# Parts of the samples' value product reordered, homes of their own for the first output weights, four bank pairs for the second layer's output

## The reference

```python
# layer 0: one input projection; branch A: GLU, causal depthwise convolution, layer norm, swish;
# branch B: attention with three parts (compressed blocks, chosen blocks, sliding window)
def nsa_block(q, g, ...):
    p_c = masked_softmax(q . kc);  o_c = p_c @ vc                 # compressed keys
    idx = top_k(score from p_c)                                    # 16 blocks of 64 keys
    p_s = masked_softmax(q . ks[idx]); o_s = p_s @ vs[idx]
    p_w = masked_softmax(q . kw, last 512); o_w = p_w @ vw
    return gq[0] * o_c + gq[1] * o_s + gq[2] * o_w
y0 = concat(A * silu(gate_a), B * silu(gate_b)) @ w_out_even      # 1024 x 1024
x1 = layer_norm(alpha * x + y0)
# layer 1: pooling mixer
v, gate = split(x1 @ w_in_odd)
d = causal window means of v (2, 4, 8, 16 tokens) - v
mixed = (d per group @ w_pool_grp) * scale
y = layer_norm(alpha * x1 + (mixed * silu(gate)) @ w_out_odd)      # 1024 x 1024
```

## Time and profile before

| | us |
|---|---|
| median of 3 runs | 1155.79 (1154.0 to 1157.73) |
| the profiled execution, its own time | 1155.27 |
| its span | 1153.5 |
| PE busy in it | 1107.2 (96%) |
| DVE, ACT, POOL busy | 739.5, 381.8, 369.4 |

### The profile page before, as it was taken

One profiled execution on the slowest core, in us unless ns is written; L12 is line 12 of the kernel. 1 busy time (PEld: TensorE's weight loads), 2 busy tenths in 40 slices (PEclk: granted clock), 3 DMA queues, 4 the chain that ended last, 5 costly groups with the idle time before them and its releaser, 6 DMA issues.

```text
span 1153.5 us, 17848 instructions
## 1 busy us (share of the span) xinstructions
PE 1107.2 (96%) x7080; PEld 918.1 (80%) x7080; DVE 739.5 (64%) x1337; ACT 381.8 (33%) x812; POOL 369.4 (32%) x376
## 2 busy tenths in 40 slices
PE   6999999999999989999999999899999999998997
PEld 6888999999988845556555556688799999997884
DVE  3677889999983598656555556556546620276745
ACT  4202111223223567766556655210121211362000
POOL 4544520000002587664754464300022221326000
PEclk9999999999999999999999999999999999998999
DMA  8653512253220122140572063722221111041321
GB/s 251 230 168 107 183 37 55 87 177 110 52 42 1 53 70 74 38 146 2 205 242 102 1 220 117 175 91 84 72 74 54 37 55 44 0 146 73 128 91 46
DMA packets 85884, 113.67 MB, mean 99 GB/s; under 512 B 21952, under 2 KB 67144, under 8 KB 85727
## 3 DMA queue, kind: packets, MB, share of 16 engines
q1 hardware_dynamic: 71849, 69.51, 19.7%
q0 software_dynamic: 11776, 41.95, 10.6%
q10 hardware_dynamic: 2182, 1.16, 0.4%
HBM read 100.91 MB, written 16.64 MB: 102 GB/s over the span
## 4 chain that ended last, share of the span: by engine, by line
PE 81%; DVE 7%; DMA 5%; POOL 3%; issue 2%; ACT 1%; SPq 1%; DVEq 0%; ACTq 0%
PE PS L697 25%; PE PS L1730 16%; PE PS L1908 15%; PE PS L1260 5%; PE PS L1246 5%; PE PS L1125 5%; PE PS L685 3%; PE PS L1163 2%; DMA RING<-in_cache_kv_sel,idx 2%; DMA WRAW<-in_w_in_even 2%; DVE PS L1342 1%; PE PS L1169 1%; DVE ACC L557 1%; PE PS L1888 1%; DMA WOR<-in_w_out_even 1%
## 5 line engine op out<-in xcount | busy, mean ns | idle before, releaser
L604 DVE SCALAR_TENSOR_TENSOR Y<-U,SM,Y 128x1024 f32<-128x1024 f32 x120 | 147.9, 1293 | 0.3
L697 PE MATMUL PS<-XH,WH 128*128 128x352 f32 (+1 forms) x648 | 146.5, 330 | 0.0
L697 PE MATMUL PS<-XL,WH 128*128 128x352 f32 (+1 forms) x648 | 143.6, 326 | 0.0
L697 PE MATMUL PS<-XH,WL 128*128 128x352 f32 (+1 forms) x648 | 142.9, 325 | 0.0
L697 PEld LDWEIGHTS PS<-XH,WH 128*128 128x128 f32 (+1 forms) x648 | 107.6, 185 | 2.7
L697 PEld LDWEIGHTS PS<-XH,WL 128*128 128x128 f32 (+1 forms) x648 | 107.9, 185 | 1.4
L697 PEld LDWEIGHTS PS<-XL,WH 128*128 128x128 f32 (+1 forms) x648 | 107.6, 185 | 1.4
L2015 POOL TENSOR_TENSOR WL<-WRAW,WH 128x1024 fp32r<-128x1024 f32 x14 | 37.8, 2698 | 216.2 <-ACT WH L1960 216.2
L557 DVE SCALAR_TENSOR_TENSOR ACC<-PS,SM,ACC 128x508 f32<-128x508 f32 x124 | 86.9, 741 | 25.1 <-PE PS L685 23.1
L288 POOL TENSOR_TENSOR WL<-WRAW,WH 128x1024 fp32r<-128x1024 f32 x12 | 28.7, 2390 | 231.8 <-ACT WH L361 231.8
L1730 PE MATMUL PS<-WOH,XH 128*128 128x512 f32 (+1 forms) x288 | 93.4, 407 | 6.3 <-DVE GT L2077 3.1
(11 more groups left out here) (319 smaller groups left out, 2065.0 us busy)
## 6 DMA issues: line engine op xcount, KB each, us to landing
WRAW<-in_w_in_even SPq DMA_DIRECT2D x16, 512.0 KB, 3.8
WRAW<-in_w_in_odd SPq DMA_DIRECT2D x16, 512.0 KB, 4.0
TM<-in_state_win_kv SPq DMA_DIRECT2D x12, 512.0 KB, 6.9
XIN<-in_x_prompt SPq DMA_DIRECT2D x8, 512.0 KB, 12.8
WRAW<-in_w_in_even SPq DMA_DIRECT2D x16, 256.0 KB, 3.8
XR<-in_x_prompt SPq DMA_DIRECT2D x8, 512.0 KB, 3.5
layer_out<-R SPq DMA_DIRECT2D x8, 512.0 KB, 2.6
XR<-layer_out SPq DMA_DIRECT2D x8, 512.0 KB, 3.3
```

The lines of the kernel that those rows point to most:

```text
L604: v.scalar_tensor_tensor(dst, src, CWT[:, i, t:t + 1], dst, ALU.mult, ALU.add).then_inc(s_cv, 1)
L697: ins = pe.matmul(PS[0:mcols, 3 * slot + c, 0:CH], w[:, slot, kk, 0:mcols], x[:, kk, c * CH:(c + 1) * CH], start=(kk == 0 and n == 0), sto ...
```

## The change

Three things. First, the six parts of "pv" are put in another order. Part 0 is now the compressed term, the window of the round's last two samples and the new tokens; parts 1 and 2 are the gathered quarters 2 and 3; part 3 is the window of the first two samples; parts 4 and 5 are the quarters gathered again. What waits for the parts moves with them: the gathers for 4 and 5 come behind parts 1 and 2, those for the next round behind parts 4 and 5, SP's reload of windows behind part 0, and that for the next round behind part 3. The planner's costs and dues are changed too. Second, the raw blocks of the first output weight get six homes (WOR0) in place of four: blocks 0 and 1 are loaded behind the last round's part 0, blocks 4 and 5 while the attention still runs, blocks 6 and 7 in the homes of 2 and 3 behind the end of it. Third, in the second layer's output a tile's banks come from four pairs, (6, 0, 2, 4), in place of two; tile 0 begins with four blocks in banks 6 and 7 without waiting for the gating, tile 1 with four in 0 and 1.

```diff
@@ attention planner
             def key_tile(b, i):
-                fill(("kt", b, i), 520, ("late", ("gather", a, i), 6000) if i < 4 else None)
+                fill(("kt", b, i), 520, ("late", ("gather", a, i), 7500) if i < 4 else ("late", ("kt", four[1], 4), 6000) if b in four[2:]
+                     else ("late", ("pv", 0, 3), 6000) if a else None)
...
             for k in range(PV_PARTS):
-                fill(("pv", a, k), (1150, 950, 1400, 950, 950, 950)[k], ("late", ("gather", a, k + 1), 6000) if k in (3, 4) else None)
+                fill(("pv", a, k), (2000, 1080, 1080, 600, 1080, 1080)[k],
+                     ("late", ("gather", a, k), 7500) if k > 3 else ("late", ("pv", a, 0), 6000) if k == 3 else None)
                 bank7[0] = None
-                if k < 2:
-                    step("POOL", "X", ("gather", a, 4 + k), 5000, ("pv", a, k))
-                if k in (3, 4) and a == 0:
-                    step("POOL", "X", ("gather", 1, k - 3), 5000, ("pv", a, k))
+                if k in (1, 2):
+                    step("POOL", "X", ("gather", a, 3 + k), 5000, ("pv", a, k))
+                if k in (4, 5) and a == 0:
+                    step("POOL", "X", ("gather", 1, k - 4), 5000, ("pv", a, k))
...
-            step("ACT", "W", ("woh", kk), 1060, ("S", NP - 1), ("late", ("pv", 1, 3 + kk // 2), 6000))
+            step("ACT", "W", ("woh", kk), 1060, ("S", NP - 1), ("late", ("pv", 1, 4 if kk > 1 else 0), 6000))
@@ pe_attention, "pv"
-                    if part in (3, 4):
-                        pe.wait_ge(s_ring[part - 3], 64 * (3 * a + 3))
-                    if part == 5:
+                    if part > 3:
+                        pe.wait_ge(s_ring[part - 4], 64 * (3 * a + 3))
+                    if part == 3:
                         for i in range(2):
                             pe.wait_ge(s_wc[i], 16 * (3 * a + 3))
...
+                    if part == 0:
+                        terms = [(22, b) for b in four] + [(n, b) for n in range(16, 20) for b in four[2:]]
+                        terms += [(n, b) for n in (20, 21) for b in four]
+                    elif part == 3:
+                        terms = [(n, b) for n in range(16, 20) for b in four[:2]]
                     else:
+                        quarter = {1: 2, 2: 3, 4: 0, 5: 1}[part]
+                        terms = [(n, b) for n in range(4 * quarter, 4 * quarter + 4) for b in four]
@@ pool_attention, gathers
                     if q >= 4:
-                        po.wait_ge(s_pvq, 5 * a + q - 3)
+                        po.wait_ge(s_pvq, 5 * a + q - 2)
...
                     elif a:
-                        po.wait_ge(s_pvq, 4 + q)
+                        po.wait_ge(*((s_pvb, 1) if q else (s_pvq, 5)))
@@ sp_windows_again
-                sp.wait_ge(s_pvq, 5 * a + 3)
+                sp.wait_ge(s_pvq, 5 * a + 1)
                 sp_windows(sp, 2 * a)
                 if a == 0:
-                    sp.wait_ge(s_pvb, 1)
+                    sp.wait_ge(s_pvq, 4)
                     sp_windows(sp, 2)
@@ output projections
-        WOR = [at("WOR0", [P, 4, D], F32, 134144), at("WOR1", [P, 4, D], F32, 164832)]
+        WOR0 = [at(f"WOR0_{i}", [P, D], F32, o) for i, o in enumerate((192480, 196576, 134144, 138240, 142336, 146432))]
+        WOR1 = at("WOR1", [P, 4, D], F32, 164832)
...
+                sp.wait_ge(s_pvq, 6)
+                block(0)
+                block(1)
+                sp.wait_ge(s_pvq, 10)
+                block(2)
+                block(3)
+                sp.wait_ge(s_pvb, 2)
                 for tt in range(2):
                     sp.dma_start(XR[0][0:ntok(tt), tt, :], RES_IN[0](tt)).then_inc(s[f"xr{tt}"], 16)
-                sp.wait_ge(s_done_attn, 1)
-                for r, t in enumerate((ln_g, ln_b)):
-                    sp.dma_start(GB[:, r, :], t[0].partition_broadcast(P)).then_inc(s["gb"], 16)
                 for kk in range(4, KT):
-                    wait_wol(sp, 0, kk - 4)
+                    if kk >= 6:
+                        wait_wol(sp, 0, kk - 4)
+                    else:
+                        wait_out(sp, 0, "woh", kk - 3)
...
+                    if kk == 5:
+                        sp.wait_ge(s_done_attn, 1)
+                        for i in range(2):
+                            wait_wol(sp, 0, i)
+                        for r, t in enumerate((ln_g, ln_b)):
+                            sp.dma_start(GB[:, r, :], t[0].partition_broadcast(P)).then_inc(s["gb"], 16)
...
-        FIRST_KK = (4, 6)
+        FIRST_KK = (4, 4)
+        OUT_BANKS = ((0, 2), (6, 0, 2, 4))
+        def out_bank(layer, tt):
+            return OUT_BANKS[layer][tt % len(OUT_BANKS[layer])]
...
-                if tt >= 2:
-                    wait_out(pe, layer, "res", tt - 1)
+                in_turn = len(OUT_BANKS[layer])
+                if tt >= in_turn:
+                    wait_out(pe, layer, "res", tt - in_turn + 1)
                 if tt == 0 and layer:
+                    part(0, range(FIRST_KK[1]))
                     pe.wait_ge(s_ge, KT - 1)
-                    part(0, range(FIRST_KK[1]))
+                    part(1, range(FIRST_KK[1]))
                     pe.wait_ge(s_ge, KT)
-                    part(1, range(FIRST_KK[1]))
```

More of the change, by code:

```diff
@@ L1198, in sample @@
                     four = range(4 * a, 4 * a + 4)
-                    quarter = {0: 2, 1: 3, 3: 0, 4: 1}.get(part)
-                    terms = [(22, b) for b in four] if part == 0 else []
-                    if quarter is not None:
-                        terms += [(n, b) for n in range(4 * quarter, 4 * quarter + 4) for b in four]
-                    elif part == 2:
-                        terms += [(n, b) for n in range(16, 20) for b in four[2:]] + [(n, b) for n in (20, 21) for b in four]
-                    else:
-                        terms += [(n, b) for n in range(16, 20) for b in four[:2]]
+                    if part == 0:
[3 more added lines that the diff above has]
+                        terms = [(n, b) for n in range(16, 20) for b in four[:2]]
+                    else:
+                        quarter = {1: 2, 2: 3, 4: 0, 5: 1}[part]
+                        terms = [(n, b) for n in range(4 * quarter, 4 * quarter + 4) for b in four]
                     for n, b in terms:
@@ L1220, in sample @@
                             p, w = PTC[0:NCS, b // 4, rows_of(b)], VCN[0:NCS, b, :]
-                        ins = pe.matmul(PS[rows_of(b), 7, 0:P], p, w, start=(n == 22), stop=(n == (19 if b in four[:2] else 7)))
+                        ins = pe.matmul(PS[rows_of(b), 7, 0:P], p, w, start=(n == 22), stop=(n == 7))
                     ins.then_inc(s_pvb if part == PV_PARTS - 1 else s_pvq, 1)
@@ L1690, in raw_out @@
         def raw_out(layer, kk):
-            return WORB[:, kk - 4, :] if layer and kk >= 4 else WOR[layer][:, kk % 4, :]
+            if layer:
+                return WORB[:, kk - 4, :] if kk >= 4 else WOR1[:, kk, :]
+            return WOR0[kk if kk < 6 else kk - 4][:, :]
         def act_out_weights(act, layer, kks=range(KT)):
@@ L1703, in dve_out_weight @@
             wait_out(v, 0, "woh", kk + 1)
-            v.tensor_tensor(WOL[:, kk, :], WOR[0][:, kk % 4, :], WOH[:, kk, :].bitcast(F32), ALU.subtract).then_inc(OUT["wod"], 1)
+            v.tensor_tensor(WOL[:, kk, :], raw_out(0, kk), WOH[:, kk, :].bitcast(F32), ALU.subtract).then_inc(OUT["wod"], 1)
         def pool_out_weights(po, layer):
@@ L1785, in dve_out @@
             for tt in range(NTT):
-                n, b0 = ntok(tt), 2 * (tt % 2)
+                n, b0 = ntok(tt), out_bank(layer, tt)
                 r, st = R[layer][0:n, tt % 3, :], BST[0:n, tt % 2, :]
```

13 lines of the change are left out of this document (5 added, 8 removed).

## The result

The changed kernel took 1149.73 us (median of 5 runs, 1146.62 to 1150.34), the kernel before 1156.36 (5 runs on the same chip, 1154.0 to 1157.73): ratio 0.994, 95% interval 0.9925 to 0.9955. It is faster, but by 6.6 us where I had forecast 13.8, and the median lies 1.7 us above my range. The profiled execution was the shortest of the five: 1146.62 us, span 1144.9, 8.6 less than before. The other four took 1.7 to 3.7 us more.

A forecast was written before the change was run, and what follows sets the result against it. TensorE (PE), 81% of the chain that ended last, bounds the kernel through waits and half clock. Gains 4.4 + 1.9 + 4.8 + 3.5 = 14.6 us, less 1.0, took 1155.27 to 1141.7; median 0.5 above: 1142 us, range 1138.5 to 1148.

The forecast's parts named there:

- Round 1: First round of the value product: waits for gathered rows and windows, and the half clock, go; gain 4.4 us.
- Round 2: Second round of the value product: the 1.41 us wait goes, the 1.26 us one shrinks to 0.5; gain 1.9 us.
- 1.0 us that I took off for small waits: Both value-product rounds: deduction for unreadable small waits for copies, some 40 instructions of each standing in a new order.
- First output projection: Its tile 0: weight block 4 ready before PE comes, 0.1 to 0.5 us wait left at block 6; gain 4.8 us.
- 16.8 us from the first cast to the first sum: First output projection: sign of success, ACT's first cast to DVE's first sum of tile 0, before 21.6 us.
- no wait at block 4: First output projection: sign of success, PE not waiting for weight block 4, where it had waited 2.96 us.
- Second output projection: Second layer's output: tile 0 starts at 1039.64 without the gating, waits 0.4 and 2.0 us stay; gain 3.5 us.
- Rival (B): Second output projection: clock falls in the new 2.0 us wait for WOL 7; 1144 to 1145 us, chance 0.17.
- seven places: From the attention on: all the places where PE was said to stand still, waits up to 2.96 us and longer.
- (C): Attention: gives nothing, since DVE, ACT and POOL are now what it waits for; 1147.5 us, chance 0.14.
- (D): First output projection: casts or the DVE and POOL port hold block 4; 4.8 us less gain, 1147, chance 0.06.
- (E): Value product, both rounds: window copies land late; 1154.6 us, chance 0.06 for no change, 0.02 for slower.

The follow-up runs named there:

- homes_alone: The kernel before with only the six homes of the first output weights and their earlier loads; 1150.86 us, ratio 0.9964 to before.
- y_behind: The changed kernel with the first output projection's first blocks of tiles 0 and 1 put behind the last value product; 1146.39 us, ratio 0.9917 to before.
- pv_alone_2: pv_alone once more, on the chip on which pv_as_planned runs; 1151.28 us, ratio 0.9969 to before.
- all_four: y_behind plus blocks 6, 7 loaded ahead of vectors, DVE's WOL 1, 3 behind last copies, second layer's tile 2 started before WOL 6, 7 waits; 1140.36 us, ratio 0.9873.
- pv_as_planned: pv_alone without the added dependency, so the planner places the first blocks of tiles 0 and 1; 1153.94 us, ratio 0.9986 to before.
- blocks_first_only: The changed kernel with only blocks 6 and 7 asked for ahead of the gain and offset vectors; 1150.96 us, ratio 0.9965 to before.
- old_banks: The changed kernel with the second layer's output back on two bank pairs; 1152.19 us, 2.0 above the changed kernel in the same set.
- pv_alone: The kernel before with only the reordered value product, first blocks of tiles 0 and 1 kept behind the last value product; 1149.95 us, ratio 0.9966 to before.

## Why the prediction was right and wrong

**Round 1: right, term mis-sized.** Predicted 4.4 us, measured 3.7 (93.13 to 89.42): PE stands 2.36 us less and is busy 1.35 less, the half clock for which I had put 1.6. The windows landed in 4.0 and 4.9 us, and neither the gathered rows nor the windows of samples 4 and 5 are waited for. Instead of the 0.4 for the final transpose and 0.3 for windows there are 0.41 at that transpose, 0.74 at a PRC transpose that waits for ACT's copy, and nothing for windows. Set against homes_alone, whose old order waited 4.01 us there, it is 6.0: what the change removes depends on when the loads of the old order land and on the half clock behind them, and one profile of the old order could not size it.

**Round 2: the term was wrong.** Predicted 1.9, measured 0.0 where the first blocks keep their place (69.15, 69.17, 69.16). The two waits of 1.41 and 1.26 are gone, and in y_behind and pv_alone_2 there are 0.44 and 0.48 for windows, 0.64 (0.63) and 0.92 for copies. I had kept 0.5 us for the copies behind DVE's output weights, and they came to 1.56. By the waits alone 0.67 us would be left; but small gaps are 0.14 more (PE stands 2.17 us in all where it stood 2.70), and the same 602 matmuls keep PE busy for 67.00 us and not 66.45. The 1.0 us that I took off for small waits in both rounds covers that. The reason for the waits at the copies is in the earlier trace rows already: one such weight takes 2.77 us on DVE beside POOL's (1.23 at 727.93 in y_behind, where POOL's is done), and it stood in front of two copies now. all_four, which moves them behind the copies, has 1.1 us less here. The Trainium skill ("SBUF — State Buffer", "SBUF: two separate sides") has a DVE operation with two inputs in SBUF wait for the whole of a GpSimd one that reads SBUF and started first. The trace agrees: in y_behind DVE's weight, begun at 703.93, ended 1.1 us behind POOL's, which had begun at 702.54.

**First output projection: the step that failed.** The prediction says that block 4 is ready "by 723.9, ahead of PE, which comes there at 725.2". It was ready at 723.4, but PE came at 719.2. The 725.2 came from the order of the kernel before, 11.1 us of first blocks behind the last value product. The planner has another order in the changed kernel, and this could be seen in the order of its instructions; I compared that order in the value product and not at its end. The cover of 1.3 us that I called thin was not the one that mattered. What I gave as the mark of this step, 16.8 us from the first cast to the first sum, came out at 16.74 and shows nothing, since the time is the chain's and not PE's: the casts themselves were 4.7 us late. The other mark, no wait at block 4, did show it. y_behind, pv_as_planned and blocks_first_only show the cause from three sides. homes_alone shows that in the old order block 4 is in time, as the term has it; its 4.8 us measured 4.4 against the profile of before and 2.5 to 3.0 against the other kernels with four homes. Behind it stood a second fault of the same term: y_behind waits 1.56 us for block 6, where I had put 0.1 to 0.5.

Why the planner did it is read from its own figures, which are no times of the chip: at 299.299 of its clock PE is free, tile 0's blocks can begin at 299.385 (130 ns behind WOL 2), the next transpose at 299.451 (130 ns behind a copy). The loop takes what can begin first, whatever its rank. 0.07 us of the plan moved 5.67 us of work, and with it the start of the casts that end the attention.

**Second output projection: the mechanism right, the size met by luck.** 3.5 predicted, 3.4 measured between the profiles, 2.1 against the other five kernels with the old pairs, 2.0 by the medians of old_banks. Tile 0 starts right behind the grouped products, the waits are 0.30 and 1.68 us (predicted 0.4 and 2.0). Rival (B), a fall of the clock in the wait for WOL 7, did not come in any of the five profiles that have this wait. The rest of the 3.4 is half clock that this one execution of the kernel before had more of.

**The places counted.** The prediction counts seven places from the attention on in which PE stands still. PE's timeline of the kernel before has more: nine waits of 0.46 to 1.91 us between 401 and 541 us, one of 1.30 at 968.24 and the one of 0.87 at 1033.59. The change touches none of them, so the sum loses nothing by it; but the clock fell behind some of them, and the difference between the changed kernel's two profiles lies there.

**The other rivals.** (C) said that the attention gives nothing and came to about 1147.5; the time is near, the reason isn't: round 1 alone gave 3.7, and the placement took 4.7 of the attention back. (D) is nearest to what happened, a late block 4 because of the casts, but I gave it the casts' time of before and 0.06. What was missing was a rival in which the planner moves a step that the diff doesn't name. (E) did not come.

The sum as measured is 3.7 + 0.1 + 3.4 = 7.2 us by the profile of before, 5.9 with the bank pairs at 2.1; the medians gave 6.6 and, in the later set, 5.8.

## What to carry to other kernels

Where a program places the work, compare the whole order before and after, at each place where a term of the sum counts on an engine being busy: the work that covers a chain must stand behind the chain's start, and 5.67 us of it in front made a wait of 4.19 us where y_behind has none. Ahead of each term ask what is late next (here block 6 behind two vectors in the same queue, and a copy behind a weight on DVE), and choose as mark of a step a span that contains the engine meant to gain, not one that the chain sets. Measure between landmarks of one trace: those of the changed kernel agreed within 0.1 us where its two executions differed by 3.1. They do so only where no late load and no fall of the clock lies between them: round 1 of the old order took 93.13 us in one profile and 95.41 in another, and a term that is read from such a stretch needs more than one profile.

## What the runs showed of the hardware

- The clock of TensorE falls in some executions and not in others at the same short wait. In all thirteen profiles PE waits 0.96 us near 475 to 479 us for a PRW transpose; behind it the granted clock fell in seven and stayed at 1.00 in six. With the fall the stretch from that transpose to the value product took 77.01 to 77.11 us (475.15 to 552.23 in before), without it 75.53 to 75.58 (475.25 to 550.78 in the changed kernel). The windows view (columns as above) of before, then of the changed kernel:

```profile
476.00:480.00 4.00, 4.00 (x25) 2.79 (x24) 1.78 (x11) 2.64 (x8) 2.41 (x6) 0.65 0.00 0
```

```profile
476.00:480.00 4.00, 4.00 (x34) 2.47 (x36) 2.38 (x17) 3.78 (x13) 2.55 (x7) 1.00 0.09 15
```

- Ten of the thirteen profiles also have a fall at 404 to 416 or at 424 to 436 us. The profiles reach the value product between 550.5 and 555.2 us with nearly the same program. For the changed kernel's two profiles the time to there is the whole difference; the runs without a profile can't be taken apart in this way.
- Behind nearly the same wait (3.08 and 3.06 us) PE worked at half clock for 6 us in one execution and for some 3.5 in another. Single waits of 1.56, 1.68 and 1.73 us left the clock at 1.00, one of 2.11 in pv_alone did not (0.72 in the 4 us from 724, 0.85 in the next). With the 0.96 above, the length of a wait alone does not tell.
- An output block of 512 KB that was asked for behind two vectors of 512 KB each in one queue, with some 2 MB more asked for behind it, came after 10.1 us in y_behind and 7.7 in the changed kernel, where a pair of windows with little beside it came in 4.0 and 4.9.
